# Attention pairs: a step's value matmuls move behind the next step's scores, and the turning of the mixed rows moves to steps 0 and 5

## What is computed

```python
def fox_attention(u, w_in, b_f, q_norm_g, k_norm_g, w_out):
    proj = u @ w_in
    q, k, v, g, fl = jnp.split(proj, [D_MODEL, 2 * D_MODEL, 3 * D_MODEL, 4 * D_MODEL], axis=-1)
    q = rms_norm(...) * (FOX_HD ** -0.5); k = rms_norm(...)      # 16 heads of 64
    f_cum = jnp.cumsum(jax.nn.log_sigmoid(fl + b_f), axis=1)
    for blk in range(sn // FOX_BLOCK):                           # 8 blocks of 128 rows
        s = q[t0:t1] @ k[:t1].T + f_cum[t0:t1, None] - f_cum[None, :t1]
        p = softmax(where(mask, s, -inf))
        outs.append(p @ v[:t1])
    return (o * jax.nn.sigmoid(g)) @ w_out
```

## Time and profile before

| | us |
|---|---|
| median of 3 runs (4393.96 to 4398.84) | 4394.46 |
| the profiled execution | 4403.27 |
| its span, first to last instruction | 4401.5 |
| PE busy in the span | 4002.6 (91%) |
| DVE busy | 2067.7 (47%) |
| POOL busy | 1889.3 (43%) |
| ACT busy | 1157.7 (26%) |
| attention loop, first step to last value matmul | 1498.5 to 2446.2 |

### The profile page before, as it was taken

One profiled execution on the slowest core, in us unless ns is written; L12 is line 12 of the kernel. 1 busy time (PEld: TensorE's weight loads), 2 busy tenths in 40 slices (PEclk: granted clock), 3 DMA queues, 4 the chain that ended last, 5 costly groups with the idle time before them and its releaser, 6 DMA issues.

```text
span 4401.5 us, 50996 instructions
## 1 busy us (share of the span) xinstructions
PE 4002.6 (91%) x18932; PEld 3242.7 (74%) x18932; DVE 2067.7 (47%) x3084; ACT 1157.7 (26%) x1880; POOL 1889.3 (43%) x742
## 2 busy tenths in 40 slices
PE   4779879999999899999998799999999878999997
PEld 3557757788877777777776577777778766888886
DVE  4673444443435545455543621111258866444446
ACT  3222122111112544343442311111131332222221
POOL 2323327654654422212220565565455556354450
PEclk9888879999999999999996799999999989999998
DMA  5311101332321101010110111111111111111110
GB/s 178 109 61 37 29 17 51 96 95 76 95 91 30 35 29 34 29 34 21 34 34 15 34 44 43 52 48 48 38 39 44 58 45 37 43 57 38 48 57 39
DMA packets 243202, 224.60 MB, mean 51 GB/s; under 512 B 12484, under 2 KB 194402, under 8 KB 242035
## 3 DMA queue, kind: packets, MB, share of 16 engines
q1 hardware_dynamic: 218673, 171.41, 12.9%
q10 hardware_dynamic: 24386, 51.22, 3.5%
HBM read 218.33 MB, written 4.26 MB: 51 GB/s over the span
## 4 chain that ended last, share of the span: by engine, by line
PE 78%; DVE 13%; ACT 4%; issue 4%; DMA 1%; ACTq 0%; SPq 0%; DVEq 0%; POOL 0%; POOLq 0%
PE PS L645 10%; PE PS L646 10%; PE PS L647 10%; PE PS L769 5%; PE PS L771 5%; PE PS L770 5%; PE PS L1082 3%; PE PS L672 3%; PE PS L673 3%; PE PS L674 3%; DVE QSQ L2349 2%; DVE ADMS L1988 1%; PE PS L1052 1%; PE PS L1067 1%; PE PS L1014 1%
## 5 line engine op out<-in xcount | busy, mean ns | idle before, releaser
L2823 POOL TENSOR_SCALAR WH<-RAW 128x1024 fp32r<-128x1024 f32 (+1 forms) x255 | 727.1, 2851 | 1441.1 <-PE PS L674 538.2
L645 PE MATMUL PS<-UH,WH 128*128 128x512 f32 (+1 forms) x2192 | 879.4, 401 | 14.6 <-ACT XR L1464 8.8
L646 PE MATMUL PS<-UL,WH 128*128 128x512 f32 (+1 forms) x2192 | 873.3, 398 | 0.0
L647 PE MATMUL PS<-UH,WL 128*128 128x512 f32 (+1 forms) x2192 | 872.6, 398 | 0.0
L2825 POOL TENSOR_TENSOR WL<-RAW,WH 128x1024 fp32r<-128x1024 f32 (+1 forms) x255 | 618.1, 2424 | 21.3
L1999 DVE TENSOR_TENSOR X<-PS,X 128x512 f32<-128x512 f32 x528 | 356.9, 687 | 476.0 <-PE PS L771 431.3
L645 PEld LDWEIGHTS PS<-UH,WH 128*128 128x128 f32 (+1 forms) x2192 | 415.3, 189 | 121.1 <-ACT XR L1464 9.6
L647 PEld LDWEIGHTS PS<-UH,WL 128*128 128x128 f32 (+1 forms) x2192 | 414.0, 189 | 104.0
L646 PEld LDWEIGHTS PS<-UL,WH 128*128 128x128 f32 (+1 forms) x2192 | 414.8, 189 | 100.8 <-issue 0.2
L769 PE MATMUL PS<-WH,HH 128*128 128x512 f32 x1024 | 406.7, 397 | 26.2 <-DVE X L1999 13.4
L771 PE MATMUL PS<-WL,HH 128*128 128x512 f32 x1024 | 401.3, 392 | 0.0
(11 more groups left out here) (350 smaller groups left out, 7108.8 us busy)
## 6 DMA issues: line engine op xcount, KB each, us to landing
RAW<-in_mlp_w_dram SPq DMA_DIRECT2D x128, 512.0 KB, 3.8
ADM<-in_ada_w_dram ACTq DMA_DIRECT2D x96, 256.0 KB, 3.2
RAW<-in_w_up_dram SPq DMA_DIRECT2D x44, 512.0 KB, 3.8
ADR<-in_ada_w_dram ACTq DMA_DIRECT2D x12, 1024.0 KB, 5.2
RAW<-in_w_down_dram SPq DMA_DIRECT2D x22, 512.0 KB, 3.5
RAW<-in_ev_w_in_dram SPq DMA_DIRECT2D x20, 512.0 KB, 4.1
RAW<-in_w_in_dram SPq DMA_DIRECT2D x20, 512.0 KB, 3.9
ADS<-in_ada_w_dram SPq DMA_DIRECT2D x8, 1024.0 KB, 17.3
```

Of the source, the lines that this page charges most:

```text
L645: pe.matmul(bank(b)[0:width], wh, xh, start=(k == 0), stop=False)
L646: pe.matmul(bank(b)[0:width], wh, xl, start=False, stop=False)
L647: mm = pe.matmul(bank(b)[0:width], wl, xh, start=False, stop=(k == NK - 1))
L2823: pool.tensor_scalar(WH[slot][:, 0:n], r[:, 0:n], 1.0, None, ALU.mult).then_inc(S("w_hi"), 1)
```

## The change

- TensorE: `values(N)` leaves step N. `values(N - 1)` is issued in step N behind `scores(N + 1)` and `fill(p + 1, n, 0)`, ahead of `turn_probs(N)`. `values(127)` follows the loop. The odd `out_unit` then stands right behind `fill(p + 1, n, 1)`.
- TensorE: `turn_out(p - 1, 0)` goes from step 1 to step 0, and `turn_out(p - 1, 1)` from step 6 to the end of step 5. For half 0 it waits for 12 outputs of its pair in place of 16.
- ACT: `out_hi(p - 1, 0)` goes from step 1 to step 0, and `out_hi(p - 1, 1)` stays in step 6 but moves ahead of `exp(N + 1)`.
- DVE: `output(N - 2)` in place of `output(N - 1)` at the head of a step; `out_lo(p - 1, 0)` from step 1 to step 0.

```diff
@@ turn_out
-                    pe.wait_ge(S("od_of"), 16 * p + 16)
+                    pe.wait_ge(S("od_of"), 16 * p + (16 if g else 12))
@@ TensorE, the loop
                         fill(p + 1, n, 0)
-                        if p and n in (1, 6):
-                            turn_out(p - 1, n // 6)
+                        if p and n == 0:
+                            turn_out(p - 1, 0)
+                        if N:
+                            values(N - 1)
                         turn_probs(N)
                         if unit is not None:
                             out_unit(p - 1, unit)
                         fill(p + 1, n, 1)
-                        values(N)
                         if unit is not None:
                             out_unit(p - 1, unit + 1)
+                        if p and n == 5:
+                            turn_out(p - 1, 1)
+                values(127)
@@ ScalarE, the loop
+                        if p and n == 6:
+                            out_hi(p - 1, 1)
                         exp(N + 1)
...
-                        if p and n in (1, 6):
-                            out_hi(p - 1, n // 6)
+                        if p and n == 0:
+                            out_hi(p - 1, 0)
@@ VectorE, the loop
-                        if N:
-                            output(N - 1)
+                        if N >= 2:
+                            output(N - 2)
...
-                        if p and n in (1, 6):
+                        if p and n in (0, 6):
                             out_lo(p - 1, n // 6)
...
+                output(126)
                 output(127)
```

## The result

The changed kernel takes 4336.91 us (median; 4326.03 to 4353.66), the kernel before 4394.21 in the same comparison. The ratio is 0.9872, 95% interval 0.9855 to 0.9890: 57 us less. Forecast were 4364 us, 30 less than before, and a range of 4333 to 4393. The direction and most of the waits came out as written; the gain is almost twice as large.

The account below looks back on a forecast made before the run. PE sets the pace, busy 867.3 of the loop's 947.7 us. Gains of 12 (pairs 1 to 6), 10 (pair 0), 4.7 (pair 7) and 5 (clock), 31.7 rounded to 31, gave 4394.5 - 31 = 4363.5, called 4364; range 4333 to 4393.

Parts of the forecast that it names:

- The waits that go: PE's waits before the value matmuls (L1082) for copies into PT: 67 us go, all but the last one's 0.9.
- The waits that come, pairs 1 to 6: New PE waits, mostly for bank 7: 6.8 us a pair against 8.9; gain 12 us in six pairs.
- Pair 0: First pair, without output units: its 7.2 us of waits go and 3 of clock loss return, 10 us gain.
- Pair 7's idle time: Last pair, at the lower clock level: waits of 13.7 us against 18.4, gain 4.7.
- The clock, pairs 1 to 6: Spells at 1.2 GHz cost 22.7 us there; 5 us taken as coming back.
- The clock, pair 7: Taken to stay at the lower level, PEclk 0.5 to 0.6, with no clock gain in the sum.
- rival B: Clock comes back widely, pair 7 included: 4313, or 4343 without pair 7; chance 0.3.
- The rule on PSUM banks: Independent matmul groups should rotate through banks; by it the change loses about 1.0 us in each of some 30 places.
- The rule on clock swings: Brief PE idling between matmul groups as PSUM is cycled makes the clock swing; by it rival D results.
- rival D: Slower: bank-7 waits of steps 3, 5, 7 and 9 throttle PE, 3.1 us a spell; 4419, chance 0.06.
- C: Rival: no clock comes back, only idle time is gained, less a few new spells; 4370 to 4392, chance 0.15.
- E: Rival: copy into PT late again for the moved values, old waits stay, bank 7's are added; 4420 to 4440, chance 0.02.

Follow-up runs that it names:

- e0: The changed kernel again, unaltered, run beside other follow-up runs on one chip: 4339.5 us, ratio 0.9884.
- e5: Changed kernel with RESID_STEPS (1, 2, 3, 5) in place of (1, 3, 5, 7), so DVE's residual work of pair 0 leaves step 7: 4333.4 us.
- e7: Changed kernel with the moved values between the even and odd output units in pair 7 alone: 4318.0 us, ratio 0.9847.
- e8: Changed kernel with pair 7's values in their old step and order, pairs 0 to 6 as changed: 4372.4 us, ratio 0.9955.
- e1: Changed kernel with only the values moved; turn_out, out_hi and out_lo back in steps 1 and 6: 4334.3 us, ratio 0.9869.
- e3: Changed kernel with values between the even and odd unit in steps with output units, DVE adding the even unit before its PT copy: 4299.4 us, ratio 0.9791.
- e4: Changed kernel with values between the units, and turn_out, out_hi and out_lo back in steps 1 and 6: 4287.8 us, ratio 0.9774.
- e6: Changed kernel with values between the units, turn_out in steps 1 and 6, and RESID_STEPS (1, 2, 3, 5): 4285.5 us, ratio 0.9761.

## Why the prediction was right, and where its sizes were off

**The waits that go: right.** All waits for the copies into PT vanished from the profiled execution; in e0's one came back, 1.2 us in pair 7. In place of the last one, which I had kept at 0.9, values(127) waits 1.2 us for DVE's output. The waits on L1082 were to drop under 5 us and stand at 9.2, all for DVE's output: 3.2 in pair 0, 1.6 in pairs 1 to 6 and 4.4 in pair 7.

**The waits that come, pairs 1 to 6: right, term by term.** Pair 4 idles 6.3 us, 6.8 forecast. Its waits are 0.9 in steps 3, 5 and 7 (1.0), 0.4 in step 4 (0.3), none in step 2 (0.2), 0.9 before turn_out (0.9), 1.6 in step 9 (1.6), and 0.47 at the pair's start plus 0.32 before scores(2) (0.8). Six pairs went from 54.9 to 42.1, 12.8 us against 12. In the pairs where DVE's remainder runs long the wait before scores(2) is 1.16, as its old counterpart was longer too.

**Pair 0: 10 forecast, 6 found.** Its stretch is 7.9 shorter, 1.8 of that the value matmuls that now count in pair 1. The old waits went, and a new one of 3.2 with a low-clock spell behind it came. The step that failed is the sentence that output(N-2) is at the head of DVE's step and values(N-1) needs it only after a scores and a fill: in pair 0 DVE's residual work of the step before stands in front of it. Without that wait (e5) pair 0 gives 12.

**Pair 7's idle time: 18.4 to 15.5, forecast 13.7.** Step 0 holds 0.47 + 3.12 = 3.6 us, as forecast. Out_lo in step 0 did cost what was estimated for step 1 (1.1 for 1.3), but the wait stands before values(0), which needs output(15) queued behind it. Two more of the kind, 1.1 in step 7 and 1.0 in step 14, were missed: they wait for DVE's output, not for PT.

**The work of PE: not in the sum, 4 to 5 us.** Pairs at full clock keep PE busy for 106.4 to 106.7 us and not 107.3, 0.6 to 0.9 a pair. The trace has a likely source: of the value groups that before were followed by scores or a unit, each spent 0.13 to 0.21 us from its last matmul to the next kind, now followed by transposes 0.11. No run tests this by itself.

**The clock, pairs 1 to 6: right in size, and a matter of chance.** PE's busy time there fell from 666.7 to 648.9 us; less some 5 of the point above, 12 to 14 came back. In e0's profiled execution of the same program it was 659.3, by the same working 2 to 4:

```profile
1598.54:2297.93 699.39, 659.30 (x3936) 542.22 (x3936) 353.44 (x708) 297.45 (x511) 175.20 (x67) 0.97 0.11 32
```

The 5 that I took, out of 0 to 22.7, lies between. The kernel before had nine spells in these pairs, five behind step 0's wait and four behind step 9's. The first of the two executions had four, e0's had nine again, but in new places: five behind the two waits of 0.9 at step 5's end, two behind the one of step 3, one each behind steps 0 and 9. Over the five executions with these waits (after, e0, e5, e7, e8) 16 of 28 spells follow step 5's end. In e1, where turn_out is not there, and in e3, e4 and e6, where the units are apart, none does, and pairs 1 to 6 have none, two, one and four spells, all behind step 0. A spell followed the pair of waits in 16 of 30 cases, and the single wait of 0.9 in steps 3 and 7 in 4 of 60. So the new pair of waits in step 5 does start spells, as weighed.

**The clock, pair 7: the term that failed.** I gave it nothing, because pair 7 had stayed low in steps 7 to 10 with hardly a wait, and named as a sign of being wrong that its PEclk leaves 0.5 to 0.6. It did: 0.63, and 0.83 in e0. e8 lies 33 us above e0 (31 by the ratios), some 6 of them the seam: some 27 of the 57 are pair 7's new order, where 4.7 were forecast. The rest, 25 to 30, is what the terms for pairs 0 to 6 add up to (27), with pair 0 giving less and the others more. e7 shows that some 20 more were to be had in pair 7. What went there were waits of 1.7 to 2.1 us in steps 6 and 11 to 14 and the 5.1 at step 0; which of them had held the clock low was not tested one by one. The steps in between were not a proof that the clock could not rise. The result is the forecast's rival B in part, priced there at 4343 without pair 7 and 4313 with it, and given 0.3.

**The rule on PSUM banks** in the Trainium skill (Perfetto Trace Analysis, section Optimizing Tensor Performance) named the weak place of this change correctly. Waits of units for bank 7 grew to 34.8 us, and e3, which puts other work between two users of that bank without another bank, took them to 9.5 and won 37 us, 21 of them idle time. **The rule on clock swings** in the Trainium skill (TensorE: Matmul & The Clock Gate, section A second HAM failure mode) would have made rival D the result. The trace agrees in part. In pairs 1 to 6, with 36 waits of up to 1.6 us at bank 7 or turn_out, such waits did start spells, but no more of them than the old waits had (four and nine against nine), and the mean PEclk was 0.99, in e0 0.97, against 0.96 before; the eight more that D needed did not come. For pair 7 it agrees: e7 shortened such waits, and the clock rose from 0.63 or 0.83 to 0.93.

**Rivals.** C is excluded by the interval, D by the sign, E by the absence of the old waits for PT.

## What to carry to other kernels

When a wait is hidden by moving work away from its place, look at what that work had been covering there: here the values had hidden bank 7's evacuation, and putting them between its two users, one step late, gave 37 us more. Look also at where short waits come to stand close behind one another: here two of 0.9 us with 0.9 of work between were followed by a spell at the low clock in about half the cases, one alone in few. Price the clock over each stage by the waits that go there, and treat a stage that ran at the low level as one that can rise, with a wide range, rather than as one that stays. When an engine's output is put off by one step, check every other job that now stands in front of it, in the first round of the loop too.

## What the runs showed that was not expected

- Pair 7 of one and the same program, with the same waits, took 107.3 us in one execution and 87.7 in another, at a mean granted clock of 0.63 and 0.83.
- The same program had four spells at 1.2 GHz in pairs 1 to 6 in one execution and nine in the other.
- DVE's 128x1024 addition X<-X,XB took 3.25 us with POOL at work on a weight tile beside it, and 1.22 in e5, where it stood at another moment with no POOL instruction beside it:

```profile
1534.04 1.22 DVE L2045 TENSOR_TENSOR X<-X,XB 128x1024 f32<-128x1024 f32 x1
```
